# Layer 1's experts: two gate products of the next expert ahead of the down product, rows gathered two experts ahead, and the last loads in another order

## The reference

```python
def expert_choice_ffn(h, w_router, w_gate, w_up, w_down):
    cap = CAPACITY_FACTOR * n // N_EXPERTS          # 2 * 1024 // 16 = 128 rows for each expert
    aff = softmax(einsum('bnd,de->bne', h, w_router))
    gate, idx = lax.top_k(swapaxes(aff, 1, 2), cap)
    xg = h[bidx, idx]
    hid = silu(einsum('becd,edf->becf', xg, w_gate)) * einsum('becd,edf->becf', xg, w_up)
    out = einsum('becf,efd->becd', hid, w_down) * gate[..., None]
    return zeros_like(h).at[bidx, idx].add(out)
```

## Time and profile before

| | |
|---|---|
| median of three runs | 3416.34 us (3415.37 to 3417.86) |
| the profiled execution, its own time | 3414.7 us |
| its span in the profile | 3413.0 us |
| PE busy | 3160.0 us, 93% |
| DVE, ACT, POOL busy | 1559.8, 1009.8, 525.1 us |
| the scaling of `y`, first to last of the 15 loop experts | 2771.0 to 3341.0 us |
| expert 15 and the end | 3341.0 to 3413.0 us |

### The profile page before, as it was taken

One profiled execution on the slowest core, in us unless ns is written; L12 is line 12 of the kernel. 1 busy time (PEld: TensorE's weight loads), 2 busy tenths in 40 slices (PEclk: granted clock), 3 DMA queues, 4 the chain that ended last, 5 costly groups with the idle time before them and its releaser, 6 DMA issues. The chain is left out here.

```text
span 3413.0 us, 52595 instructions
## 1 busy us (share of the span) xinstructions
PE 3160.0 (93%) x19496; PEld 2216.1 (65%) x19496; DVE 1559.8 (46%) x3170; ACT 1009.8 (30%) x2323; POOL 525.1 (15%) x639
## 2 busy tenths in 40 slices
PE   6999989999987999999999799899899299999996
PEld 4888856667435788787887565666664155555553
DVE  3212178778654010101101254566785666666565
ACT  4111156755330111101111152235554222222222
POOL 0010235110100101011110120254101101111112
PEclk9999999999987999999999899999999599999998
DMA  6336353053639977787777630100414589999996
GB/s 231 130 108 114 92 188 113 20 132 95 241 132 339 352 267 250 244 275 245 265 255 262 232 121 1 56 22 28 112 33 173 197 293 334 326 335 339 338 335 257
DMA packets 340390, 672.38 MB, mean 197 GB/s; under 512 B 84041, under 2 KB 133065, under 8 KB 334017
## 3 DMA queue, kind: packets, MB, share of 16 engines
q1 hardware_dynamic: 308384, 568.00, 47.9%
q0 software_dynamic: 13616, 47.32, 5.5%
q10 hardware_dynamic: 18240, 55.16, 4.3%
HBM read 585.65 MB, written 90.97 MB: 198 GB/s over the span
## 5 line engine op out<-in xcount | busy, mean ns | idle before, releaser
L2756 PE MATMUL experts_gu_ps<-experts_xT,experts_wg 128*128 128x160 f32 x2048 | 301.3, 300 | 2.6 <-DVE experts_xT L2630 2.6
L2756 PE MATMUL experts_gu_ps<-experts_xT,experts_wu 128*128 128x160 f32 x2048 | 299.4, 299 | 0.0
L2756 PEld LDWEIGHTS experts_gu_ps<-experts_xT,experts_wg 128*128 128x128 f32 x2048 | 287.9, 191 | 9.9 <-issue 9.9
L2756 PEld LDWEIGHTS experts_gu_ps<-experts_xT,experts_wu 128*128 128x128 f32 x2048 | 285.6, 190 | 0.0
L2653 DVE TENSOR_TENSOR experts_hid<-experts_sil,experts_gu_ps 128x160 f32<-128x160 f32 x128 | 41.1, 321 | 516.1 <-ACT experts_sil L2584 516.1
L2722 PE MATMUL experts_y_ps<-down_ahead_wd,experts_hid 128*128 128x512 f32 x512 | 228.3, 599 | 0.0
L2584 ACT ACTIVATE experts_sil<-experts_gu_ps 128x160 f32<-128x160 f32 x128 | 38.9, 304 | 604.9 <-PE experts_gu_ps L2756 604.9
L2722 PEld LDWEIGHTS experts_y_ps<-down_ahead_wd,experts_hid 128*128 128x128 f32 x512 | 94.6, 190 | 114.4 <-issue 113.7
L3458 PE MATMUL front_pb_ps<-kept_hT,front_ahead_w 128*128 128x512 f32 (+1 forms) x384 | 138.7, 521 | 0.7 <-DVE kept_dt L3509 0.7
L3167 PE MATMUL experts_w_ps<-experts_wd,experts_hT 128*128 128x512 f32 x256 | 130.8, 597 | 8.5 <-issue 7.8
L3167 PE MATMUL experts_v_ps<-experts_wd,experts_hT 128*128 128x512 f32 x256 | 129.6, 592 | 0.0
(11 more groups left out here) (561 smaller groups left out, 6308.7 us busy)
## 6 DMA issues: line engine op xcount, KB each, us to landing
experts_wg<-in_l_w_gate SPq DMA_DIRECT2D x64, 2048.0 KB, 8.5
experts_wu<-in_l_w_up SPq DMA_DIRECT2D x64, 2048.0 KB, 12.7
down_ahead_wd<-in_l_w_down SPq DMA_DIRECT2D x32, 2048.0 KB, 10.6
experts_wd<-in_l_w_down SPq DMA_DIRECT2D x32, 2048.0 KB, 7.7
down_ahead_wd<-in_l_w_mod SPq DMA_DIRECT2D x16, 1024.0 KB, 9.2
proj<-proj_ob ACTq DMA_DIRECT2D x60, 256.0 KB, 2.3
first_w<-in_l_w_in SPq DMA_DIRECT2D x6, 2048.0 KB, 10.1
attn_a_mod_w<-in_l_w_mod ACTq DMA_DIRECT2D x12, 1024.0 KB, 6.5
```

What stands on the lines that cost most here:

```text
L2756: mm = nc.tensor.matmul(GU[f % 2][:, part, 0:N], w[:, h, k, c * P:(c + 1) * P], xT[:, k, :], start=(k == 0), stop=(k == KD - 1))
```

## The change

The order of the seven products becomes 5, 1, 2, 4, 6, 3, 7. Products 5 and 1 of the next expert's gate are issued ahead of the down product, one after each half of `turn_hidden`; for expert 0 they stand ahead of the loop. The next expert's rows are turned among the up products, after product 4, and ACT copies them in two halves between its `keep`s. They are gathered two experts ahead, after the addition's indirect DMA in POOL's queue (a 17th gather repeats expert 0's rows). DVE forms the gate's sum 5 and the first row sum between the up quarters, and all other sums, the up matrix's 5 to 7 among them, after the last quarter. SP loads both halves of a gate or up weight after product 7. In expert 15 the first four blocks of `moe` are loaded ahead of the stream rows, and two blocks are gated ahead of the end instead of four. In the scan the band's loads are issued one stored block earlier.

```diff
--- before.py
+++ after.py
@@ -2775,7 +2775,7 @@
...
 
-PRODUCTS = (5, 1, 2, 6, 3, 7, 4)
+PRODUCTS = (5, 1, 2, 4, 6, 3, 7)
 KEPT = (5, 1, 6, 7)
...
@@ -2868,14 +2868,11 @@
...
                         sp.wait_ge(mm_done, multiplied(e, i, 7))
-                        load(i, 0, e + 1)
-                        sp.wait_ge(mm_done, multiplied(e, i, 4))
-                        load(i, 1, e + 1)
+                        for half in range(2):
+                            load(i, half, e + 1)
                     for half in range(2):
...
                         load(DOWN, half, e + 1)
-                sp.wait_ge(mm_done, multiplied(E - 1, GATE, 4))
-                following.load_rows(sp, x)
                 sp.wait_ge(s_done, (E - 1) * 16)
...
@@ -2885,6 +2882,8 @@
...
                     load_sum(t)
+                sp.wait_ge(mm_done, multiplied(E - 1, GATE, 7))
+                following.load_rows(sp, x)
                 for t in range(NTX):
...
@@ -2906,21 +2905,22 @@
...
                 pool.wait_ge(choice.weighed, START + 1)
+                gather(1)
                 with pool.Fori(0, E - 1) as e:
...
                     nc.gpsimd.tensor_copy(wt[:], choice.weight[:, bass.ds(e, 1)]).then_inc(ixs_in, 1)
-                    gather(e + 1)
                     pool.wait_ge(ya, START + e + 1)
...
                     pool.indirect_dma_start(moe, bass.IndirectOffsetOnAxis(ap=ixs[:, 0:1], axis=0), y[:], None, compute_op=ALU.add).then_inc(s_done, 16)
+                    gather(e + 2)
                     pool.wait_ge(s_done, e * 16 + 16)
...
                 pool.indirect_dma_start(y[:], None, moe, bass.IndirectOffsetOnAxis(ap=ixs[:, 0:1], axis=0)).then_inc(rows_in, 16)
-                pool.wait_ge(tp_done, START + E)
+                pool.wait_ge(g_done, (E + 1) * 16)
                 pool.indirect_dma_start(xg[:], None, following.res, bass.IndirectOffsetOnAxis(ap=ixs[:, 0:1], axis=0)).then_inc(rows_in, 16)
...
@@ -2939,9 +2939,9 @@
...
             def _(act):
-                def transposed(e):
+                def transposed(e, half):
                     act.wait_ge(tp_done, START + e + 1)
-                    for k in range(KD):
+                    for k in range(half * HALF, (half + 1) * HALF):
                         a = nc.scalar.activation(xT[:, k, :], TP[k // 4][:, k % 4, :], ACT.Identity, bias=shift[:, k:k + 1], scale=gain[:, k:k + 1])
...
@@ -2957,17 +2957,21 @@
...
 
-                def gates_and_up(e, squares=()):
+                def gates_and_up(e, last=False):
                     nc.scalar.activation(unused[:], K.eps[:, 0:1], ACT.Silu)
-                    for p in KEPT:
+                    for p in KEPT[2:]:
                         keep(e, GATE, p)
...
                         if p in (1, 6):
-                            for t in squares[p // 6 * 2:p // 6 * 2 + 2]:
-                                square(t)
+                            if last:
+                                square(p // 6 * 2)
+                                square(p // 6 * 2 + 1)
+                            else:
+                                act.wait_ge(mm_done, multiplied(e, UP, 4))
+                                transposed(e + 1, p // 6)
                     for c in range(2):
...
@@ -2975,16 +2979,22 @@
...
 
+                def first_kept(e):
+                    for p in KEPT[:2]:
+                        keep(e, GATE, p)
+
                 act.sem_inc(act_out, 4)
                 act.wait_ge(vec_done, START + 1)
-                transposed(0)
+                for half in range(2):
+                    transposed(0, half)
+                first_kept(0)
                 with act.Fori(0, E - 1) as e:
                     gates_and_up(e)
-                    transposed(e + 1)
+                    first_kept(e + 1)
                     act.wait_ge(ixs_in, START + e + 1)
...
                     nc.scalar.activation(y[:, 0:BANK], Y[0][:], ACT.Copy, scale=wt[:]).then_inc(ya, 1)
-                gates_and_up(E - 1, tuple(range(4)))
+                gates_and_up(E - 1, last=True)
                 for t in range(4, NTX):
...
@@ -2997,26 +3007,29 @@
...
 
-                def row_sums(e):
+                def row_sums(e, first):
 
                     a11, a12, a21, a22 = (xT[:, k * HALF:(k + 1) * HALF, c * HD:(c + 1) * HD] for c in range(2) for k in range(2))
-                    dve.wait_ge(xa, START + e + 1)
-                    nc.vector.tensor_tensor(sx[:, 0], a21, a22, ALU.add).then_inc(sx_done, 1)
-                    nc.vector.tensor_tensor(sx[:, 3], a11, a21, ALU.subtract).then_inc(sx_done, 1)
-                    dve.wait_ge(sx_done, START + e * 4 + 1)
-                    nc.vector.tensor_tensor(sx[:, 1], sx[:, 0], a11, ALU.subtract).then_inc(sx_done, 1)
-                    dve.wait_ge(sx_done, START + e * 4 + 3)
-                    nc.vector.tensor_tensor(sx[:, 2], a12, sx[:, 1], ALU.subtract).then_inc(sx_done, 1)
+                    if first:
+                        dve.wait_ge(xa, START + e * 2 + 2)
+                        nc.vector.tensor_tensor(sx[:, 0], a21, a22, ALU.add).then_inc(sx_done, 1)
+                    else:
+                        after(dve, mm_done, e * 14)
+                        nc.vector.tensor_tensor(sx[:, 3], a11, a21, ALU.subtract).then_inc(sx_done, 1)
+                        dve.wait_ge(sx_done, START + e * 4 + 1)
+                        nc.vector.tensor_tensor(sx[:, 1], sx[:, 0], a11, ALU.subtract).then_inc(sx_done, 1)
+                        dve.wait_ge(sx_done, START + e * 4 + 3)
+                        nc.vector.tensor_tensor(sx[:, 2], a12, sx[:, 1], ALU.subtract).then_inc(sx_done, 1)
 
...
                     if p == 5:
-                        for half in range(2):
-                            dve.wait_ge(w_in[i][half], START + e * 16 + 16)
+                        dve.wait_ge(w_in[i][0], START + e * 16 + 16)
                         add = nc.vector.tensor_tensor(sums_of(i, 5), b12, b11, ALU.subtract)
...
                         dve.wait_ge(sums_done[i], START + e * 4 + 1)
+                        dve.wait_ge(w_in[i][1], START + e * 16 + 16)
                         add = nc.vector.tensor_tensor(sums_of(i, 6), b22, sums_of(i, 5), ALU.subtract)
...
@@ -3039,23 +3052,29 @@
...
 
-                def gates_and_up(e, between=None):
-                    weight_sum(e, GATE, 4)
-                    weight_sum(e, UP, 5)
-                    quarter(e, GATE, 0)
-                    quarter(e, GATE, 1)
-                    weight_sum(e, UP, 6)
-                    quarter(e, GATE, 2)
-                    quarter(e, GATE, 3)
-                    weight_sum(e, UP, 7)
+                def gates_and_up(e, last=False):
+                    for q in range(4):
+                        quarter(e, GATE, q)
                     weight_sum(e, UP, 4)
...
                     for q in range(4):
-                        if between and q in (0, 2):
-                            between(q)
-                            between(q + 1)
+                        if q == 1 and last:
+                            for t in range(2):
+                                gated(t)
+                        elif q == 1:
+                            weight_sum(e + 1, GATE, 5)
                         quarter(e, UP, q)
                         hidden(e, q)
+                        if q == 1 and not last:
+                            row_sums(e + 1, True)
+
+                def rest_of_sums(e):
+                    weight_sum(e, GATE, 6)
+                    weight_sum(e, GATE, 7)
+                    row_sums(e, False)
+                    weight_sum(e, GATE, 4)
+                    for p in (5, 6, 7):
+                        weight_sum(e, UP, p)
 
...
@@ -3073,24 +3092,21 @@
...
                 weight_sum(0, GATE, 5)
-                weight_sum(0, GATE, 6)
-                row_sums(0)
-                weight_sum(0, GATE, 7)
+                row_sums(0, True)
+                rest_of_sums(0)
                 with dve.Fori(0, E - 1) as e:
                     gates_and_up(e)
-                    for p in (5, 6, 7):
-                        weight_sum(e + 1, GATE, p)
-                    row_sums(e + 1)
+                    rest_of_sums(e + 1)
                     dve.wait_ge(ixs_in, START + e + 1)
...
                 dve.wait_ge(gate_done, START + 1)
-                gates_and_up(E - 1, gated)
+                gates_and_up(E - 1, last=True)
                 dve.wait_ge(following.x_in, START + 16 * NTX)
                 for t in range(NTX):
-                    if t >= M_SLOTS:
+                    if t >= 2:
                         gated(t)
...
@@ -3169,13 +3185,19 @@
...
                 turn_rows(0)
+                for p in PRODUCTS[:2]:
+                    multiply(0, GATE, p)
                 with pe.Fori(0, E - 1) as e:
-                    for i in (GATE, UP):
-                        for p in PRODUCTS:
-                            multiply(e, i, p)
+                    for p in PRODUCTS[2:]:
```

(17 more changed lines are left out.)

## The result

The changed kernel takes **3428.18 us** (median, 3424.78 to 3432.83) against 3416.47 us (3413.71 to 3420.16) for the kernel before on the same chip: ratio 1.0036, 95% interval 1.0025 to 1.0047, so about 11.7 us slower. The forecast was 3421.6, + 5.3: the right sign, inside the range, and less than half of the size. The likeliest class, no change that can be told, was missed.

A forecast was written before the change was run, and what follows sets the result against it. PE was taken to bound the loop, with transfers close behind. Loop + 8.1, first expert + 3.8, end - 8.3 and band + 1.7 summed to + 5.3, so 3421.6 us; range 3412.0 to 3430.0.

The forecast's parts named there:

- The wait for W: Loop: product 2 waits until ACT has scaled bank W, starting 1.05 us after D, the end of the down product.
- The 0.77 that goes: Loop: PE's idle 0.68 ahead of the down product and 0.09 behind it disappear, 0.77 us an expert.
- the term for the changes: Loop: changes between products and transposes cost 0.18 us more going in and 0.12 coming out, per expert.
- The first expert: Expert 0: later sums + 0.7, products 5 and 1 first + 3.45, gap and changes - 0.68 + 0.30; + 3.8 us.
- The end: After the last scaling: `moe` blocks load first, PE's stall vanishes, `summed` starts when the stream rows land; - 8.3 us.
- the two `gated`: End, in the bound of - 5: two `gated` operations now behind the rows cost 1.2 us each.
- The band: End of the scan: a store queues behind the band's earlier loads, so the next stage opens later; + 1.7 us.
- (a): End: DVE sets it, as two `gated` behind the rows aren't hidden; 2.4 us more, 3424.0; chance 0.14.
- (b): Loop: weights land beyond the 1.2 us cover, 14 us per microsecond; at 0.5 late, 3428.6; chance 0.10.
- (c): Loop: the wait for bank W isn't paid, 12.6 us less, 3409.0; chance 0.08.
- (d): Expert 15: PE still ends last and its whole gain of 17.6 us counts, 3412.3; chance 0.05.
- (e): End of the scan: the band's loads gain 1.9 us after all, 3418.0; chance 0.07.

The follow-up runs named there:

- the kernel with the order alone: Kernel before, only SP's loads of the first four `moe` blocks issued ahead of the next stream rows: 3408.68 us, ratio 0.9974.
- the kernel with the rows first: Changed kernel with the stream rows loaded ahead of the first four `moe` blocks again in expert 15: 3434.79 us, single run.
- the three edits together: Changed kernel with gate order 5, 1, 6, 3, 2, 4, 7, both hidden transposes behind product 5, band's loads put back: 3411.29 us, ratio 0.9988.

## Why the prediction was right in sign and short in size

**The loop, + 8.1 forecast, + 15.4 measured.** The wait for W was right: 1.05 forecast, 1.00 measured, ACT starting 0.26 after D, and taken away it gives 0.90 back. The 0.77 that goes is gone. The step that failed is the term for the changes, + 0.18 and + 0.12, 0.30 in all. By subtraction it is 1.10 - 1.00 + 0.77 = 0.87 (1.10 is what the step grew by); summed from the rows, 1.09 in the changed kernel and 0.05 in product 2, less 0.28 that the kernel before paid already (0.09 into `ht` and 0.06 in its first four, 0.50 to `tp` for 0.44; 0.05 in product 5; 0.08 in the down product's first pair, 1.10 for 1.02), 0.86. Three things were wrong in it: I took changes out of transposes as nearly free, by a change from `tp` to `ht` which is 128 columns wide on both sides and so no change at all, while the true one in the rows, 0.09 from the down product to product 5, stood only under what goes; I left out that product 1 now stands directly ahead of the down product; and I let the time of the first matmuls behind a change (1.95 for 1.90, 1.10 for 1.02, 0.66 for 0.60), which stood in the rows of before, pass as rounding. The Trainium skill, "TensorEngine Tiling (Array Packing)", section "Key Properties", says that a change of the tiling mode, not just of the tile, drains TensorE. The runs agree with it as far as they go: a pair of changes cost 0.31, and `tp` to `ht` in the earlier trace rows nothing (the row of eight is 0.44 longer than that of four behind it, 1.04 and 0.60). I had not weighed it, though it speaks against just this change. That a drain is what the 0.15 each way consists of, no run shows.

**The first expert, + 3.8 forecast, + 4.3 measured** (from the first row sum to the first scaling, 43.8 and 48.1). DVE's sums held the up products by 0.62 (0.7 forecast). The rest is the same mis-sized term once more, 0.87 for 0.30.

**The end, - 8.3 forecast, - 5.9 measured.** By their mean share the DMA engines ran empty 30.9 after the last scaling, as forecast (30.7). I let `summed` start in that moment. It started 1.9 later, and 1.3 later in the kernel with the order alone (3372.3 by the share of 0.16 in 2 us, start at 3373.62). The mean was the wrong reading: `summed` waits for the last of the rows, and one or the other engine ends later than the mean says. In the kernel with the order alone that accounts for most of the 1.3, as data still moved after 3373.0:

```profile
3373.00:3373.50 0.50, 0.50 (x2) 0.19 (x1) 0.00 (x0) 0.00 (x0) 0.00 (x0) 1.00 0.02 8
```

In the changed kernel 1.3 to 1.8 remain behind the last data; why so much more, no run shows. The rows of before couldn't show such a distance, since PE was late there. The bound of a microsecond was too small for it; that - 5.9 still lies between - 9.3 and - 5 is owed to the two `gated`, which cost 0.3 at most of the 2.4 that the bound gave them. The other 0.5 lies in the emptying (0.2) and behind the first `summed` (33.3 for 33.0).

**The band, + 1.7 forecast, + 1.6 measured** at the keys; the stage opened 7.17 after the block of 2399.05, against 4.22 before, 2.95 later (2.7 forecast). That the size came out so well is luck: in the other four profiles with the moved loads the stretch to the keys is 2.4 to 2.8 longer than before. The mechanism was right, the store waits behind the loads. Of the rule of the Trainium skill in "DMA: Bandwidth & Descriptors", section "Queues, rings and completion order", the half by which the store waits holds here (4.66 to 5.87 with the loads ahead, 0.76 to 0.80 without), and no overtaking showed. I had read the other half too short: that section of the Trainium skill adds that a transfer's semaphore rises only after every earlier write of that DMA engine, and the slot is released by the semaphore.

The four measured parts make 15.4 + 4.3 - 5.9 + 1.6 = 15.4, 2.3 more than the spans differ and beyond the 13.5 of my upper bounds added up. The 2.3 lie in other stretches: the scan's block ahead of the band came 1.7 earlier (2399.05, 2400.77), and 0.6 lies between the keys and the first row sum. The 1.7 is no more than chance: the kernel with the rows first, the same program up to there, has that block at 2401.45. So it is in part luck that the time lies inside the range.

**The signs that I had named.** Three came out against me: the step is 41.81 and not 41.2 to 41.4; DVE waits for `wg` in the loop, 1.70, though without cost; and 66.1 from the last scaling to the end is just over 63 to 66. The wait for W, the gap ahead of the down product that is gone, `summed` and the band's opening came out as named.

**The rivals.** (a) fell: DVE's two moved operations cost 0.3 at most. (b) fell: DVE started on the gate's half at D + 17.8 (landing forecast at 17.7), having waited for it, and 1.39 us were left where I had said 1.2. (c) fell to the wait of 1.00. (d) fell: the rows ended last. (e) fell to the slot's 4.66. No rival named the true miss, dearer changes. It was inside my forecast's own bounds (5.0 to 11.3 for the loop) in kind, but those let a change out of transposes cost 0.1 at most, and the loop lay 4 us beyond their upper end.

## What to carry to other kernels

Count the changes of matmul width that a reordering brings, and price them by what the trace has at a true change of width; work moved ahead of a product to fill a gap of 0.7 us can bring more than that in changes. The first product behind a shared PSUM bank pays its read-out, so put there a product that writes another bank: 0.90 us a step here. Where a wait counts many transfers together, split it by what the first consumer needs: that and the order of the loads gave 0.38%, and the loop's edits, with the wait for W and one pair of changes taken out again, gave nothing (40.70 for 40.71).

## What the runs showed of the hardware

- A change from 64-column products to 128-column matmuls cost 0.10 us and 0.05 to 0.06 more in the first transposes behind it (0.10 in the first pair of the down product); the way back cost 0.09 and 0.05 in the product behind it. One more pair made the step 0.31 longer.
- From the moment at which the DMA engines were empty by their mean share to the start of the waiting VectorE operation it took 1.9 and 1.3 us with transfers of 0.5 MB. From the last data it took 1.3 to 1.8 and 0.1 to 0.6, since the engines didn't end together.
- A store behind 1.15 MB of small pieces, in the queue that SP issues, released its slot 4.66 to 5.87 us after the next block was ready (five profiles), against 0.76 to 0.80 ahead of them (five).
- PE's granted clock was 1.00 (2.4 GHz) from 3390 to 3392 in the changed kernel, during a down product with no stall of 11.45 us ahead of it, and 0.50 (1.2 GHz) in the earlier trace rows, within that stall. In the three edits together it was 0.50 from 3370 to 3372, behind stalls of 3.04 and 0.75 us; in the changed kernel the stalls ahead of the down product were 1.67 and 0.75.
